# Query-key products over 128 rows with zeroed query rows, in place of products over 64 rows

## Chip, core and metric

The kernel runs on one NeuronCore of a Trainium2 chip, as one program. The metric is the device time of an execution in microseconds (us). The core has five engines with a queue each: PE (TensorE, matrix products; its weight loads are shown as PEld), DVE (VectorE), ACT (ScalarE), POOL (GpSimd) and SP (SyncE, which issues the transfers here). They meet by semaphores only.

## What is computed

Three transformer layers in a row over 512 tokens of width 1024, all in float32. The first two have the same form: a norm, an input projection, two kinds of attention side by side, an output projection, and a gated feed-forward block. The third mixes stick-breaking attention with a gated recurrence. What matters here are the query-key products:

```python
# differential attention: 4 heads, each with 2 maps m of width 64
logits = jnp.einsum('bqhmd,bkhmd->bhmqk', qi, k) * scale
p = softmax(where(causal, logits, NEG_INF))
p = p[:, :, 0] - lam * p[:, :, 1]
# forgetting attention: 8 heads of width 64, with a decay added to the logits
logits = jnp.einsum('bqhd,bkhd->bhqk', qi, k) * scale + decay
# stick-breaking attention, third layer: 8 heads of width 64
z = jnp.einsum('bhtd,bhsd->bhts', qb, kb) * scale
```

A head of width 64 fills half of the 128 partitions. The two maps of a differential head, and two neighbouring stick-breaking heads, lie above each other in one 128-row tile.

## The kernel before

Each engine has its own program, written out by hand, and its order is the order of its queue. Projections are made of three float32r products for each tile (`three`, lines 1291 to 1296): weights come by DMA into `raw`, ACT rounds them into `w_hi`, POOL subtracts into `w_lo`, and PE multiplies. This stream fills PE nearly everywhere.

**Attention of the first two layers** (`attention1` on PE, ACT and DVE). First 24 items are transposed (`items1`, `transpose_item`, line 1440): for each of four differential heads a query item into `QAT` and a key item into `KAT`, then queries and keys of the eight forgetting heads, with 66 rows each (64 and two for the decay). ACT takes the even items, the queries, out of PSUM (line 649), DVE the odd ones (line 1002). Six banks of PSUM rotate, and PE waits for an item's evacuation before it uses its bank again; after item 7 come the forget gate's sums.

Then 64 units (`units1`) run as a pipeline. The first 32 are differential, in the order head, block `i` of 128 queries, map `m`; the other 32 are forgetting, in the order head, block. At step `u` PE does three things in this order: it transposes the probabilities of unit `u - 5` (line 1489, only for `m == 1` in differential heads); it makes the query-key product of unit `u` (line 1501, `128 * (i + 1)` columns) and adds the causal mask to it with a bf16 product of the identity (line 1503); and it multiplies the transposed probabilities of unit `u - 6` by the values (line 1513). A differential query-key product takes partitions `64 * m` to `64 * m + 64` of both operands; the mask, the transposes and the value products take all 128, and a forgetting query-key product takes 66. For each unit DVE finds the maxima (line 1023), ACT takes the exponentials (line 673) and copies the transposed probabilities to SBUF (line 660), and DVE joins the two maps (lines 1030 to 1033) and scales the output (line 1018). The query-key products rotate over four banks.

**Stick-breaking attention** lies inside the input projection of the third layer. `SIDE` lists what is woven into each quarter lap of the projection: eight turned items (`items2`: queries to `QST`, keys to `KST`), then 32 units (`units2`) of a head and a block of keys. Each unit's query-key product (line 1576) takes 64 partitions of both operands and `512 - 128 * j` columns; it stands between products of the projection, which take 128.

Of the kernel before, what the change touches and what calls it, by code (L numbers as in the profile page):

```python
# [25 lines left out]
ALU = mybir.AluOpType  # L26
ACT = mybir.ActivationFunctionType
AX = mybir.AxisListType

P = 128  # L30
SEQ = 512
# [7 lines left out]
HD = 64  # L39
# [93 lines left out]
def build(nc, x, positions, attn_pre_g, w_in, forget_bias, lam_q1, lam_k1, lam_q2, lam_k2, diff_sub_g,  # L133
# [4 lines left out]
    with ctx:  # L138
        def sb(name, shape, dt=F32, scope=ctx):
            return scope.enter_context(nc.sbuf_tensor(name, shape, dt))  # L140
# [16 lines left out]
        G = sb("G", [P, D])  # L157
        gcol = sb("gcol", [P, 10, KD])
        qkg = sb("qkg", [P, 2])
        cs = sb("cs", [P, 2, T, ROT])  # L160
        fw = sb("fw", [P, DEPTH, KD, 16], F32R)
        fbias = sb("fbias", [P, DEPTH, 8])
# [30 lines left out]
        def at2(a, *dims):  # L193
            return view(R2, a, dims)
# [12 lines left out]
        QA = at2(0, T, CW)  # L207
        KA = at2(2048, T, CW)
# [2 lines left out]
        QB = at2(6160, T, 8, 66)  # L211
        KB = at2(8272, T, 8, 66)
        VB = at2(10384, T, 8, 65)
        QAT = at2(12464, 4, SEQ)
        KAT = at2(14512, 4, SEQ)
        prob = at2(16560, PROBS, SEQ)
        probT = at2(20144, 2, SEQ)
# [6 lines left out]
        YG_down = at1(0, T, D)  # L224
        junk_down = at1(4096, T, CW)

        QST, KST = at2(4096, 4, SEQ), at2(6144, 4, SEQ)
        VS = at2(8192, T, CW)
        QS, KS = at2(10240, T, CW), at2(12288, T, CW)
        SQ2 = at2(15872, T, CW)  # L230
# [110 lines left out]
        items1 = []  # L341
        for h in range(4):
            cols = slice(h * P, (h + 1) * P)
            items1 += [(QA[:, :, cols], P, QAT[:, h, :], HD ** -0.5), (KA[:, :, cols], P, KAT[:, h, :], 1.0)]
        for h in range(8):
            items1 += [(QB[:, :, h, :], 66, QBT[0:66, h, :], HD ** -0.5), (KB[:, :, h, :], 66, KBT[0:66, h, :], 1.0)]
        items2 = []
        for h in range(4):
            cols = slice(h * P, (h + 1) * P)
            items2 += [(QS[:, :, cols], P, QST[:, h, :], qkg[:, 0:1]), (KS[:, :, cols], P, KST[:, h, :], qkg[:, 1:2])]  # L350

        units1 = [("diff", (h, m), i) for h in range(4) for i in range(T) for m in range(2)]
# [178 lines left out]
        def _(act):  # L532
# [96 lines left out]
            nc.scalar.activation(cs[:, :, :, :], ang[:, 4:6], ACT.Sin).then_inc(trig_done, 1)  # L629
            act.preload_act_table_set(EXP_TABLE)  # L630

            def attention1(l):
                stage = f"in{l}"

                with act.Fori(2 if l == 0 else 1, LAPS[stage]) as lap:
                    hi_lap(stage, LAP0[stage] + lap)
                hi_first(f"out{l}")

                act.wait_ge(f_mm, l + 1)
                nc.scalar.activation(f_rows, PS[0:16, 0, :], ACT.Copy).then_inc(f_copied, 1)  # L640
                act.wait_ge(f_biased, l + 1)
                link(nc.scalar.activation(fy[:, 1], fy[:, 0], ACT.Abs))
                link(nc.scalar.activation(fy[:, 1], fy[:, 1], ACT.Exp, scale=-1.0))
                nc.scalar.activation(fy[:, 1], fy[:, 1], ACT.Ln, bias=1.0).then_inc(f_log, 1)

                for n, (src, rows, dst, scale) in enumerate(items1):
                    if n % 2 == 0:
                        act.wait_ge(tr_mm, len(items1) * l + n + 1)
                        nc.scalar.activation(dst, PS[0:rows, 2 + n % 6, :], ACT.Copy, scale=scale).then_inc(tr_act, 1)

                b, bo, bj = len(units1) * l, n_out * l, n_join * l
                for u in range(len(units1) + TURN):
                    v = u - TURN
                    if v >= 0 and has_output[v]:
                        i = units1[v][2]
                        n = outputs(v)
                        act.wait_ge(pt_mm, bo + n)
                        if bo + n > 2:
                            act.wait_ge(o_mm, bo + n - 2)
                        nc.scalar.activation(probT[:, n % 2, 0:P * (i + 1)], PS[:, 4 + n % 2, 0:P * (i + 1)],  # L660
                                             ACT.Copy).then_inc(pt_ev, 1)
                    if u < len(units1):
                        kind, (h, m), i = units1[u]
                        act.wait_ge(max_done, b + u + 1)
                        if u >= PROBS and has_output[u - PROBS]:
                            act.wait_ge(pt_mm, bo + outputs(u - PROBS))
                        elif u >= PROBS:
                            act.wait_ge(joined, bj + joins(u - PROBS + 1))
                        elif l and u == 0:
                            act.wait_ge(pt_mm, bo)  # L670

                        sums_to = dict(accum_out=dsum[:, (u // 2) % 8, m:m + 1]) if kind == "diff" else {}
                        nc.scalar.activation(prob[:, u % PROBS, 0:P * (i + 1)], PS[:, u % 4, 0:P * (i + 1)], ACT.Exp,
                                             bias=nmax[:, u % 4:u % 4 + 1], **sums_to).then_inc(exp_done, 1)
                    if u == DIFF_ROOT:
                        act.wait_ge(ss_ready, l + 1)
                        first_root(16, 2 * HD)
# [61 lines left out]
                nc.scalar.activation(w_hi[:, r], raw[:, r], ACT.Copy).then_inc(hi_ready, 1)  # L739

            def turn_side(n):
                src, rows, dst, scale = items2[n]
                if n % 2 == 0:
                    act.wait_ge(tr_mm, 2 * len(items1) + n + 1)
                    nc.scalar.activation(dst, PS[:, 4 + n % 4, :], ACT.Copy, scale=scale).then_inc(tr_act, 1)

            def sb_side(u):
                v = u - 3
# [95 lines left out]
        def _(dve):  # L844
            V = nc.vector
# [67 lines left out]
            for l in range(DEPTH):  # L913
                link(V.tensor_scalar(gcol[:, 3 * l + 1, 0:1], gcol[:, 3 * l + 1, 0:1], 1.0 - LAM_INIT[l], None, ALU.mult))
                V.tensor_copy(gcol[:, 3 * l + 1, 1:4], gcol[:, 3 * l + 1, 0:1].to_broadcast([P, 3]))
            V.tensor_scalar(qkg[:, 0:1], qkg[:, 0:1], HD ** -0.5, None, ALU.mult)
            link(V.tensor_copy(fw[:, :, :, 0:8], fw_raw))
            V.tensor_tensor(fw[:, :, :, 8:16], fw_raw, fw[:, :, :, 0:8].bitcast(F32), ALU.subtract).then_inc(fw_done, 1)

# [369 lines left out]
        def _(pe):  # L1289
# [153 lines left out]
            def attention1(l):  # L1443
# [33 lines left out]
                for u in range(len(units1) + PRODUCT):  # L1477
                    v = u - TURN
                    if 0 <= v < len(units1) and has_output[v]:
                        i = units1[v][2]  # L1480
                        n = outputs(v)
                        if units1[v][0] == "diff":
                            pe.wait_ge(joined, bj + joins(v))
                        else:
                            pe.wait_ge(exp_done, b + v + 1)
                        if bo + n > 2:
                            pe.wait_ge(pt_ev, bo + n - 2)
                        for j in range(i + 1):
                            last = nc.tensor.transpose(PS[:, 4 + n % 2, j * P:(j + 1) * P],  # L1489
                                                       prob[:, v % PROBS, j * P:(j + 1) * P], ident[:, :])  # L1490
                        last.then_inc(pt_mm, 1)
                    if u < len(units1):
                        kind, (h, m), i = units1[u]
                        tok, upto = slice(i * P, (i + 1) * P), P * (i + 1)
                        if kind == "diff":
                            q, kk = QAT[64 * m:64 * m + 64, h, tok], KAT[64 * m:64 * m + 64, h, 0:upto]
                        else:
                            q, kk = QBT[0:66, h, tok], KBT[0:66, h, 0:upto]
                        if b + u >= 4:
                            pe.wait_ge(exp_done, b + u - 3)  # L1500
                        mm(PS[:, u % 4, 0:upto], q, kk, start=True, stop=False)  # L1501

                        mm(PS[:, u % 4, upto - P:upto], ident_b[:, :], causal_b[:, :], start=False, stop=True).then_inc(s_mm, 1)  # L1503
                    v = u - PRODUCT
                    if v >= 0 and has_output[v]:
                        kind, (h, m), i = units1[v]
                        n = outputs(v)
                        pe.wait_ge(pt_ev, bo + n)
                        if bo + n > 2:
                            pe.wait_ge(o_norm, bo + n - 2)  # L1510
                        for j in range(i + 1):
                            vals, width = (VA[:, j, h * P:(h + 1) * P], P) if kind == "diff" else (VB[:, j, h, :], HD + 1)
                            last = mm(PS[:, 6 + n % 2, 0:width], probT[:, n % 2, j * P:(j + 1) * P], vals,  # L1513
                                      start=j == 0, stop=j == i)
                        last.then_inc(o_mm, 1)
# [50 lines left out]
            def sb_steps(u):  # L1566
# [3 lines left out]
                if u < len(units2):  # L1570
                    h, j = units2[u]
                    n = SEQ - P * j
                    rows = slice(64 * (h % 2), 64 * (h % 2) + 64)
                    if u >= 2:
                        pe.wait_ge(sp_done, u - 1)
                    mm(PS[:, 4 + u % 2, 0:n], KST[rows, h // 2, j * P:(j + 1) * P], QST[rows, h // 2, j * P:SEQ],  # L1576
                       start=True, stop=True).then_inc(z_mm, 1)
                yield
                v = u - 2
# [168 lines left out]
```

## Time and profile before

| | us |
|---|---|
| median of 3 runs | 2375.33 |
| the three runs | 2368.23, 2375.33, 2383.04 |
| the profiled execution, device time | 2381.19 |
| its span in the profile | 2379.4 |
| differential units, first layer | 173.4 to 220.1 |
| differential units, second layer | 872.3 to 938.2 |
| stick-breaking units | 1508 to 1672 |

A profile names groups of instructions by line, engine and operands; "64*128 64x512" on a PE line is a product that contracts over 64 rows, with 512 moving columns. A float32 product appears as two records ("x2"). The ends of PE's records are modelled, so lengths are read here from one start to the next start. The granted clock is TensorE's clock as a share of its full 2.4 GHz: 1.00 is 2.4 GHz and 0.50 is 1.2 GHz.

### The profile page before, as it was taken

What the parts mean: (1) busy time and instruction counts of PE and PEld (TensorE: products, weight loads), DVE (VectorE), ACT (ScalarE), POOL (GpSimd) and SP (SyncE); (2) the same over time, 40 slices, a digit from 0 to 9 for tenths busy, and PEclk for the clock granted to TensorE, in tenths of its full rate; (3) what the DMA queues carried; (4) which work ended last, traced back from release to release, by engine and by line L of the source; (5) the groups of instructions that cost most, each with busy time, mean ns of one, the idle gap of its engine ahead of it and who ended that gap; (6) DMA issues with size and microseconds to landing.
All of it is one profiled execution on the core that took longest, in us unless ns stands there. A gap on an engine that the chain in (4) does not pass through costs nothing.

```text
span 2379.4 us, 27399 instructions
## 1 busy us (share of the span) xinstructions
PE 2282.4 (96%) x10268; PEld 1775.5 (75%) x10268; DVE 716.9 (30%) x1374; ACT 736.9 (31%) x1217; POOL 842.7 (35%) x390
## 2 busy tenths in 40 slices
PE   7999999999989999999999999999798899999999
PEld 6876778888877865778888877777566677888887
DVE  5126442112022035542122023444466432212200
ACT  4135442222232134442222223444322243222211
POOL 3430134444434420134444434323334233444442
PEclk9998999999999986999999999999999999999999
DMA  5320023233232310023323322211111122332332
GB/s 162 97 63 1 28 80 98 88 97 93 93 97 80 89 44 1 19 81 97 97 89 97 92 92 74 62 45 53 39 43 44 45 75 77 96 97 88 97 93 93
DMA packets 138734, 178.20 MB, mean 75 GB/s; under 512 B 19856, under 2 KB 87696, under 8 KB 138640
## 3 DMA queue, kind: packets, MB, share of 16 engines
q1 hardware_dynamic: 137024, 175.25, 24.5%
q10 hardware_dynamic: 1616, 1.64, 0.2%
q8 instruction: 65, 1.06, 0.2%
q14 instruction: 29, 0.24, 0.0%
HBM read 174.76 MB, written 2.10 MB: 74 GB/s over the span
## 4 chain that ended last, share of the span: by engine, by line
PE 40%; issue 36%; POOL 18%; DVE 3%; ACT 1%; DMA 1%; POOLq 0%; SPq 0%; ACTq 0%; DVEq 0%
POOL w_lo L475 18%; PE PS L1294 8%; PE PS L1295 8%; PE PS L1296 8%; PE PS L1501 4%; PE PS L1513 3%; PE PS L1588 1%; DVE R L1206 1%; PE PS L1663 1%; PE PS L1489 1%; PE PS L1576 1%; PE PS L1440 1%; PE PS L1300 1%; PE PS L1602 1%; PE PS L1503 1%
## 5 line engine op out<-in xcount | busy, mean ns | idle before, releaser
L475 POOL TENSOR_TENSOR w_lo<-raw,w_hi 128x1024 fp32r<-128x1024 f32 (+1 forms) x288 | 676.9, 2351 | 1068.6 <-ACT w_hi L550 1068.6
L550 ACT ACTIVATE w_hi<-raw 128x1024 fp32r<-128x1024 f32 (+1 forms) x291 | 303.2, 1042 | 1075.5 <-DMA raw<-in_w_up 329.5
L1294 PE MATMUL PS<-xt_hi,w_hi 128*128 128x512 f32 x1120 | 450.9, 403 | 3.4 <-DVE xt_lo L886 3.4
L1295 PE MATMUL PS<-xt_lo,w_hi 128*128 128x512 f32 x1120 | 445.1, 397 | 0.0
L1296 PE MATMUL PS<-xt_hi,w_lo 128*128 128x512 f32 x1120 | 444.5, 397 | 0.0
L1294 PE MATMUL PS<-w_hi,xt_hi 128*128 128x512 f32 x928 | 389.3, 419 | 11.7 <-DVE xt_lo L886 8.4
L1295 PE MATMUL PS<-w_lo,xt_hi 128*128 128x512 f32 x928 | 370.7, 399 | 0.0
L1296 PE MATMUL PS<-w_hi,xt_lo 128*128 128x512 f32 x928 | 370.5, 399 | 0.0
L1294 PEld LDWEIGHTS PS<-xt_hi,w_hi 128*128 128x128 f32 x1120 | 211.7, 189 | 60.0 <-issue 10.8
L1296 PEld LDWEIGHTS PS<-xt_hi,w_lo 128*128 128x128 f32 x1120 | 211.8, 189 | 51.3
L1295 PEld LDWEIGHTS PS<-xt_lo,w_hi 128*128 128x128 f32 x1120 | 212.0, 189 | 48.4
L1084 DVE TENSOR_TENSOR h_tmp<-silu_g,PS 128x512 f32<-128x512 f32 x66 | 45.4, 687 | 581.6 <-ACT silu_g L710 580.5
L1294 PEld LDWEIGHTS PS<-w_hi,xt_hi 128*128 128x128 f32 x928 | 177.2, 191 | 58.1 <-issue 17.5
L1294 PE MATMUL PS<-w_hi,ht_hi 128*128 128x512 f32 x528 | 209.2, 396 | 5.6 <-POOL w_lo L475 5.6
L1296 PEld LDWEIGHTS PS<-w_hi,xt_lo 128*128 128x128 f32 x928 | 176.7, 190 | 43.2
L1296 PE MATMUL PS<-w_hi,ht_lo 128*128 128x512 f32 x528 | 208.5, 395 | 0.0
L1295 PE MATMUL PS<-w_lo,ht_hi 128*128 128x512 f32 x528 | 208.5, 395 | 0.0
L1295 PEld LDWEIGHTS PS<-w_lo,xt_hi 128*128 128x128 f32 x928 | 177.4, 191 | 37.2 <-issue 2.2
L469 POOL TENSOR_TENSOR w_lo<-raw,w_hi 128x1024 fp32r<-128x1024 f32 x40 | 99.0, 2476 | 133.1 <-ACT w_hi L739 125.4
L1294 PEld LDWEIGHTS PS<-w_hi,ht_hi 128*128 128x128 f32 x528 | 99.0, 187 | 32.1 <-POOL w_lo L475 8.2
L1296 PEld LDWEIGHTS PS<-w_hi,ht_lo 128*128 128x128 f32 x528 | 99.0, 187 | 24.2
L1501 PE MATMUL PS<-R 64*128 64x256 f32 (+7 forms) x256 | 115.3, 538 | 1.7 <-DVE R L1002 0.9
(215 smaller groups left out, 2136.5 us busy)
## 6 DMA issues: line engine op xcount, KB each, us to landing
raw<-in_w_in SPq DMA_DIRECT2D x92, 512.0 KB, 3.7
raw<-in_w_gate SPq DMA_DIRECT2D x88, 256.0 KB, 2.8
raw<-in_w_up SPq DMA_DIRECT2D x88, 256.0 KB, 3.0
raw<-in_w_down SPq DMA_DIRECT2D x40, 512.0 KB, 3.8
raw<-in_w_out SPq DMA_DIRECT2D x24, 512.0 KB, 3.8
raw<-in_w_ffn_gate SPq DMA_DIRECT2D x44, 256.0 KB, 2.8
raw<-in_w_ffn_up SPq DMA_DIRECT2D x44, 256.0 KB, 3.0
raw<-in_w_ffn_down SPq DMA_DIRECT2D x20, 512.0 KB, 3.8
```

The costliest lines, as they stand in the source:

```text
L469: nc.gpsimd.tensor_tensor(w_lo[:, r], raw[:, r], w_hi[:, r].bitcast(F32), ALU.subtract).then_inc(lo_ready, 1)
L475: nc.gpsimd.tensor_tensor(w_lo[:, r, 0:subs, :], raw[:, r, 0:subs, :], w_hi[:, r, 0:subs, :].bitcast(F32), ALU.subtract).then_inc(lo_ready, 1)
L550: nc.scalar.activation(w_hi[:, r, 0:subs, :], raw[:, r, 0:subs, :], ACT.Copy).then_inc(hi_ready, 1)
L1084: V.tensor_tensor(h_tmp[:, :], silu_g[:, j, :], PS[:, 4 * s + 2 + j, :], ALU.mult).then_inc(h_mul, 1)
L1206: V.tensor_reduce(hg_at[:, v % 2, :], hg_a.rearrange("p l t -> p t l"), AX.X, ALU.add).then_inc(a_sum, 1)
L1294: mm(out_, a_hi, b_hi, start=start, stop=False)
L1295: mm(out_, a_hi, b_lo, start=False, stop=False)
L1296: return mm(out_, a_lo, b_hi, start=False, stop=stop)
L1300: ins = nc.tensor.transpose(PS[:, 4 + k % 4, t * P:(t + 1) * P], SOURCE[stage][:, t, k * P:(k + 1) * P], ident[:, :])
L1440: last = nc.tensor.transpose(PS[0:rows, bank, t * P:(t + 1) * P], src[:, t, :], ident[:, :])
L1501: mm(PS[:, u % 4, 0:upto], q, kk, start=True, stop=False)
L1513: last = mm(PS[:, 6 + n % 2, 0:width], probT[:, n % 2, j * P:(j + 1) * P], vals, start=j == 0, stop=j == i)
```

## The change

Every query-key product of the differential and stick-breaking heads takes all 128 partitions. The keys of both maps (or both heads) stay above each other as they are. The queries are kept twice, in two buffers: buffer `m` holds the queries of map or head `m` in its 64 rows and zeros in the others. The zeros come from the scale of the copy out of PSUM: `one_head` holds a column for each `m` with the scale in its own rows and 0.0 in the others, so ACT copies each query item twice, with a column each. That makes 4 more ACT copies of 128x512 in each of the first two layers and 4 more in the third. `one_head` is filled by DVE in the preparation at the start (five instructions in place of one). Each product keeps its number of columns and of weights.

```diff
+        one_head = sb("one_head", [P, 2, 2])
-        QAT = at2(12464, 4, SEQ)
+        QAT = (at2(12464, 4, SEQ), at2(23216, 4, SEQ))
-        QST, KST = at2(4096, 4, SEQ), at2(6144, 4, SEQ)
+        QST = (at2(4096, 4, SEQ), at2(24064, 4, SEQ))
+        KST = at2(6144, 4, SEQ)
-            items1 += [(QA[:, :, cols], P, QAT[:, h, :], HD ** -0.5), (KA[:, :, cols], P, KAT[:, h, :], 1.0)]
+            items1 += [(QA[:, :, cols], P, [q[:, h, :] for q in QAT], one_head[:, 0, :]), (KA[:, :, cols], P, KAT[:, h, :], 1.0)]
-            items2 += [(QS[:, :, cols], P, QST[:, h, :], qkg[:, 0:1]), (KS[:, :, cols], P, KST[:, h, :], qkg[:, 1:2])]
+            items2 += [(QS[:, :, cols], P, [q[:, h, :] for q in QST], one_head[:, 1, :]), (KS[:, :, cols], P, KST[:, h, :], qkg[:, 1:2])]
+            def turned_out(item, bank):
+
+                src, rows, dst, scale = item
+                if not isinstance(dst, list):
+                    return nc.scalar.activation(dst, PS[0:rows, bank, :], ACT.Copy, scale=scale)
+                for m in range(2):
+                    last = nc.scalar.activation(dst[m], PS[:, bank, :], ACT.Copy, scale=scale[:, m:m + 1])
+                return last
-                        nc.scalar.activation(dst, PS[0:rows, 2 + n % 6, :], ACT.Copy, scale=scale).then_inc(tr_act, 1)
+                        turned_out(item, 2 + n % 6).then_inc(tr_act, 1)
-                    nc.scalar.activation(dst, PS[:, 4 + n % 4, :], ACT.Copy, scale=scale).then_inc(tr_act, 1)
+                    turned_out(items2[n], 4 + n % 4).then_inc(tr_act, 1)
-            V.tensor_scalar(qkg[:, 0:1], qkg[:, 0:1], HD ** -0.5, None, ALU.mult)
+            link(V.memset(one_head[:, :, :], 0.0))
+            for m in range(2):
+                rows = slice(HD * m, HD * m + HD)
+                link(V.memset(one_head[rows, 0, m:m + 1], HD ** -0.5))
+                link(V.tensor_scalar(one_head[rows, 1, m:m + 1], qkg[rows, 0:1], HD ** -0.5, None, ALU.mult))
-                            q, kk = QAT[64 * m:64 * m + 64, h, tok], KAT[64 * m:64 * m + 64, h, 0:upto]
+                            q, kk = QAT[m][:, h, tok], KAT[:, h, 0:upto]
-                    rows = slice(64 * (h % 2), 64 * (h % 2) + 64)
-                    mm(PS[:, 4 + u % 2, 0:n], KST[rows, h // 2, j * P:(j + 1) * P], QST[rows, h // 2, j * P:SEQ],
+                    mm(PS[:, 4 + u % 2, 0:n], KST[:, h // 2, j * P:(j + 1) * P], QST[h % 2][:, h // 2, j * P:SEQ],
```

## Rows read from the trace of the kernel before

**Rows 1.** page, section 2: granted TensorE clock in 40 slices of the span, tenths of full speed.

```profile
PEclk9998999999999986999999999999999999999999
```

**Rows 2.** windows by stage; columns: length, busy us per engine, granted clock, DMA share, GB/s.

```profile
173.40:220.10 46.70, 46.25 (x191) 25.65 (x192) 29.53 (x86) 23.38 (x75) 0.00 (x0) 0.85 0.00 1
872.30:938.20 65.90, 65.84 (x191) 35.47 (x192) 30.36 (x86) 24.00 (x75) 0.00 (x0) 0.56 0.00 1
220.10:270.00 49.90, 48.98 (x355) 39.31 (x353) 33.71 (x111) 29.86 (x72) 7.63 (x5) 1.00 0.00 1
...
1508.00:1672.00 164.00, 164.00 (x729) 115.83 (x729) 68.11 (x148) 72.23 (x143) 51.18 (x48) 1.00 0.17 49
```

**Rows 3.** windows of 1 us, PE only: where the granted clock falls and rises.

```profile
178.00:179.00 1.00, 1.00 (x4) 0.70 0.00 0
...
192.00:193.00 1.00, 1.00 (x5) 0.97 0.00 0
...
874.00:875.00 1.00, 1.00 (x4) 0.86 0.00 0
...
932.00:933.00 1.00, 1.00 (x2) 0.63 0.00 0
```

**Rows 4.** timeline of PE: start us, length us; differential heads, first layer, full clock.

```profile
197.98 0.48 PE L1501 MATMUL PS<-R 64*128 64x128 f32 x2
198.39 0.23 PE L1503 MATMUL PS<-causal_b,ident_b 128*128 128x128 bf16 x1
198.55 0.48 PE L1501 MATMUL PS<-R 64*128 64x128 f32 x2
...
205.98 0.27 PE L1489 MATMUL PS<-ident,R 128*128 128x128 f32 x1
206.18 1.12 PE L1501 MATMUL PS<-R 64*128 64x512 f32 x2
...
209.11 0.48 PE L1501 MATMUL PS<-R 64*128 64x128 f32 x2
```

**Rows 5.** the same timeline, forgetting heads (66 rows), full clock.

```profile
225.40 0.39 PE L1501 MATMUL PS<-R 66*128 66x128 f32 x2
225.62 0.22 PE L1503 MATMUL PS<-causal_b,ident_b 128*128 128x128 bf16 x1
225.68 0.28 PE L1489 MATMUL PS<-ident,R 128*128 128x128 f32 x1
225.79 0.60 PE L1501 MATMUL PS<-R 66*128 66x256 f32 x2
```

**Rows 6.** timeline of PE, differential heads, second layer, half clock.

```profile
884.45 0.79 PE L1501 MATMUL PS<-R 64*128 64x128 f32 x2
885.17 0.29 PE L1503 MATMUL PS<-causal_b,ident_b 128*128 128x128 bf16 x1
...
903.95 0.79 PE L1501 MATMUL PS<-R 64*128 64x128 f32 x2
```

**Rows 7.** timeline of PE, stick-breaking product between projection products.

```profile
1561.52 0.49 PE L1576 MATMUL PS<-R 64*128 64x128 f32 x2
1561.93 0.50 PE L1294 MATMUL PS<-xt_hi,w_hi 128*128 128x512 f32 x1
```

**Rows 8.** timeline of all engines at the end of a head, first layer.

```profile
197.32 0.23 PE L1503 MATMUL PS<-causal_b,ident_b 128*128 128x128 bf16 x1
...
198.99 0.37 ACT L660 ACTIVATE R<-PS 128x256 f32<-128x256 f32 x1
...
199.42 0.71 PE L1513 MATMUL PS<-R 128*128 128x128 f32 x4 [0.22 <-ACT R L660]
```

**Rows 9.** timeline, evacuation of the first eight transposed items, first layer.

```profile
162.30 2.04 ACT L649 ACTIVATE R<-PS 128x512 f32<-128x512 f32 x4
...
162.61 2.47 DVE L1002 TENSOR_SCALAR R<-PS 128x512 f32<-128x512 f32 x4
```

**Rows 10.** timeline, evacuation of the last turned query item before stick-breaking.

```profile
1505.25 0.69 ACT L745 ACTIVATE R<-PS,qkg 128x512 f32<-128x512 f32 x1 [2.96 <-PE PS L1440]
```

More of the change, by code:

```diff
@@ L644, in attention1 @@
                 nc.scalar.activation(fy[:, 1], fy[:, 1], ACT.Ln, bias=1.0).then_inc(f_log, 1)
-                for n, (src, rows, dst, scale) in enumerate(items1):
+                for n, item in enumerate(items1):
                     if n % 2 == 0:
                         act.wait_ge(tr_mm, len(items1) * l + n + 1)
-                        nc.scalar.activation(dst, PS[0:rows, 2 + n % 6, :], ACT.Copy, scale=scale).then_inc(tr_act, 1)
+                        turned_out(item, 2 + n % 6).then_inc(tr_act, 1)
                 b, bo, bj = len(units1) * l, n_out * l, n_join * l
@@ L741, in turn_side @@
             def turn_side(n):
-                src, rows, dst, scale = items2[n]
                 if n % 2 == 0:
                     act.wait_ge(tr_mm, 2 * len(items1) + n + 1)
-                    nc.scalar.activation(dst, PS[:, 4 + n % 4, :], ACT.Copy, scale=scale).then_inc(tr_act, 1)
+                    turned_out(items2[n], 4 + n % 4).then_inc(tr_act, 1)
             def sb_side(u):
```

## The prediction

> **What bounds the kernel now.** I read the page's row of granted clock first. [rows 1] Most slices stand at 9; the drops that last are slice 4 (8) and slices 15 and 16 (8 and 6) of 40, each 59.5 us long. They fall in the differential units of the two layers. Then I read the windows by stage. [rows 2] The differential units take 46.7 us in the first layer at a mean clock of 0.85, and 65.9 us in the second at 0.56: the same 32 units, the same 191 PE instructions, 19 us apart. PE is busy in nearly all of both, while DVE is busy for 29.5 and ACT for 23.4 of the 46.7 us. So PE sets the pace, and in part its clock. The forgetting units behind them run at 1.00, and so does the whole stick-breaking stretch, where PE is busy for 164.00 of 164 us: there every nanosecond taken from PE's stream is taken from the end.
>
> The windows of one microsecond date the clock. [rows 3] A slice whose mean is 0.70 holds 0.6 us at the 0.50 level, so the clock fell at 178.4 and, from the 0.97, rose at 192.1. In the second layer (0.86 and 0.63) it fell at 874.7 and rose at 932.7. PE was at half clock for 13.7 and 58.0 us. Both falls come within 5 us of the first differential product, when there are query-key products and masks and hardly anything between them. Both rises come amid differential units that are like the ones before.
>
> Last I read PE's timeline, which gives the price of one 64-row product.
>
> **The change part by part.** *Full clock, differential.* From a 64-row product of 128 columns to its mask is 0.41 us; from the mask to the next 64-row product 0.16; from a transpose to one 0.20. [rows 4] In the forgetting heads the same steps take 0.22, 0.06 and 0.11. [rows 5] Those products have the same columns and type, the same mask behind them, and differ in their 66 rows. So a 64-row product costs 0.19 us on its way out and 0.10 on its way in, say 0.30 together.
>
> The change makes all products 128-row ones. I price them as the 66-row ones; the other bound is that they keep the 0.30 (the third rival below). The Trainium skill, "TensorEngine Tiling (Array Packing)", Key Properties, states that changing the tiling mode drains the TensorE; by it 128-row products among 128-row ones have no drain left and the bound falls away. The trace agrees in that the extra time lies at both borders of a 64-row product. A unit then saves 0.30, a head of eight units 2.4 of its 11.13 us [rows 4], a layer of 32 units 9.6.
>
> A rule that speaks against the change: "TensorE: Matmul & The Clock Gate", Part 3 of the Trainium skill, says that small products in distinct row groups run at once. If the two maps did so before, the change would end it and lose half of a head's eight products: 2.2 us, by 0.22 for 128 columns, and 18 in all. The trace shows none of it: the second map's product starts 0.16 us after the mask, which waits for the first. [rows 4]
>
> *What takes the place of the drains.* PE isn't far ahead of the others at the end of a head. After the 512-column pair a value product waited for ACT's copy: the mask began at 197.32, the copy ran from 198.99, the product began at 199.42. [rows 8] That chain (maximum, exponential, copy) is 2.1 us and doesn't shorten. In front of that product PE has two 128-column units and thereby two drains, 0.6 us, that vanish and come back as waiting. Hence 1.8 saved a head in place of 2.4; I take 9.3 us for a head. Bounds: 8.7 if the chain hides, and some 10 if DVE, with 29.5 us of work a layer against 31.4 for PE, delays other units too.
>
> *The clock.* A head at half clock takes 19.50 us [rows 6] against 11.13, so 43% of the time at half clock is loss: 5.9 us of 13.7 and 24.9 us of 58.0. Taken off, the stages are 40.8 and 41.0 us; that they agree backs the reading. What will the clock do after? Forgetting units, without drains, never lost it in 50 us. [rows 2] It fell only where 64-row products made up most of PE's work. After the change that first stretch is denser and full-height. I take full clock in both layers; the other bound is the same half-clock time as now. The skill's page "TensorE: Matmul & The Clock Gate", Part 1, says that the gate follows how busy the array is. The trace agrees only if busy isn't the record's sense, since PE's busy share was 1.00 in the very slices of the falls. [rows 3]
>
> At full clock a stage is then 41.0 - 9.6 + 4 x 0.6 = 33.8 us. The first layer saves 46.7 - 33.8 = 12.9, the second 65.9 - 33.8 = 32.1.
>
> *Stick-breaking.* A 64-row product of 128 columns holds PE for 0.41 us until the projection's next product. [rows 7] That is the 0.19 again over 0.22, and I take the 0.10 of the entry with it: 0.30 x 32 = 9.6 us. PE is busy throughout, so all of it reaches the end. Bounds: 6, if the side chain on DVE and ACT then holds PE at some units, and 10.
>
> *What is added.* In each of the first two layers ACT has four more copies of 0.51 us. [rows 9] Its first eight items' share then ends at 162.30 + 8 x 0.51 = 166.4 rather than 164.3, DVE's at 165.1. What is late next is the bank of item 0, freed 0.5 us later, for which PE's item 6 waits, and the gate's sums behind it. DVE's 165.1 hides part of that: 0.4 us a layer, 0.8 together; nothing if it is all hidden, 2.04 a layer if none. In the third layer each extra copy is 0.6 to 0.7 us, and ACT was idle for 2.96 us before such a copy [rows 10]: nothing, and 4 x 0.69 = 2.8 without that cover. ACT's rounding of weights queues behind it, but the rounding runs three slots ahead of PE. The five small DVE instructions at the start lie before a copy that PE needs only a lap later: nothing; some 2 us if the next copy were due. No transfer is added or moved.
>
> *Sum.* 12.9 + 32.1 + 9.6 - 0.8 = 53.8 us. From the profiled execution's 2381.2 that leaves 2327.4. The median was 5.9 us lower than this execution. I don't subtract that: the runs differ by 15 us with the same work, most likely in their time at half clock, which the forecast takes away anyway. If it lay elsewhere, the result would be 2321.5. **Forecast 2327.**
>
> **Rivals.**
> *The clock behaves as now.* The falls came early and the rises at no visible event, which speaks for a habit of the stage. The forgetting stretches at 1.00 speak against. At half clock a product's way out is 0.72 us [rows 6], against 0.44 for twice 0.22: 0.28, with 0.10 in, 0.38 a unit. The second layer saves 32 x 0.38 = 12.2, the first 8.5 (32 x 0.30, 0.7 more for nine units at half clock, 1.8 less for the waits of three heads); with 9.6 - 0.8 that is 29.5. Here the median is the right base: 2375.3 - 29.5 = 2346.
> *Waiting takes the place of every drain in the differential stages*, because DVE's and ACT's chains bind. For it: the wait in [rows 8] and DVE's 29.5 us. Against it: they leave 4 us in 33.8. A stage is 41.0, so 2327.4 + 2 x 7.2 = 2342.
> *The price isn't that of 64 rows*, but of something that both kernels share, such as the wider value products; then only the added copies are left: 2376. Against it, stick-breaking shows the same 0.41 without them. [rows 7]
> *Slower.* With waits in PE's stream in place of drains, the array is less active, the clock falls in both differential stages and stays down in the forgetting ones. The stages are 65.9 - 12.2 = 53.7 each, which costs 7.0 and saves 12.2; with 8.8 more, 14.0 saved. The two forgetting stretches of 50 us grow by 75%: +75. That gives 2381.2 - 14.0 + 75 = 2442. It decides from about 19 us of forgetting work at half clock. Against it: those stretches never fell, and aren't changed.
>
> **How the numbers follow.** Full clock 0.71, clock as now 0.14, waits for drains 0.08, no price 0.03, slower 0.04. The likeliest case's own range is 2318 to 2337: 8.7 or 10 us a head (-5, +6), the added copies (up to +5), stick-breaking (+3), the median's offset (-6). The range 2319 to 2349 takes in the waiting case and most of the clock case. A measurement of this kernel tells about 1% from no change, here 24 us, so faster ends at 2351.6. Faster: 0.71, two thirds of the clock case (0.09) and 0.07 of the waits: 0.87. Within 1%: 0.05 + 0.01 + 0.03 = 0.09. Slower: 0.04.
>
> **What would show it.** Line 1501 as 128*128 with 0.22 us from product to mask and 0.06 behind it; granted clock 1.00 over both stages; both stages near 34 us and equal; more waits of the value products for ACT's copy; 32 stick-breaking products with 0.22 in place of 0.41 and the stretch near 154 us. It is wrong if the 1 us windows still show 0.50 for tens of microseconds, if product to mask stays at 0.41, or if the evacuation before the units grows by over 1 us.

## The result, and the profile after

| | before | changed |
|---|---|---|
| median, us | 2379.18 (4 runs, 2368.23 to 2384.3) | 2279.82 (4 runs, 2276.68 to 2281.47) |
| span of the profiled execution, us | 2379.4 | 2279.2 |
| differential units, first layer | 46.73 | 34.29 |
| differential units, second layer | 65.84 | 34.28 |
| stick-breaking, first product to last | 149.75 | 137.05 |

The ratio is 0.958, with a 95% interval of 0.9538 to 0.9621: faster, by 99 us. The forecast was 2327, and its range ended at 2319. The direction was right and the size wrong: 54 us were foreseen, and some 45 more came.

The page of the changed kernel, section 2, shows the clock's slices answering to [rows 1]:

```profile
PEclk9999999999999999999999999999999999999999
```

The drops in slices 4, 15 and 16 are gone. The windows by stage of the changed kernel (length, busy us of PE, PEld, DVE, ACT and POOL with counts, granted clock, DMA share, GB/s) answer to [rows 2]; the last is the stick-breaking stretch and the work just behind it:

```profile
169.60:203.90 34.30, 32.00 (x191) 22.71 (x192) 28.59 (x86) 22.31 (x74) 0.00 (x0) 1.00 0.00 1
841.80:876.10 34.30, 31.98 (x191) 22.71 (x192) 28.58 (x86) 22.30 (x74) 0.00 (x0) 1.00 0.00 1
1433.60:1585.00 151.40, 151.40 (x731) 120.23 (x730) 68.60 (x148) 71.66 (x143) 51.97 (x48) 1.00 0.17 53
```

Both differential stages now take the same 34.3 us at full clock. In the stick-breaking stretch PE is busy without a break, as before, and from its first product to its last it takes 137.05 us in place of 149.75. The timeline of PE in the second differential head of the first layer (start us, length us) answers to [rows 4]:

```profile
174.85 0.22 PE L1517 MATMUL PS<-causal_b,ident_b 128*128 128x128 bf16 x1
...
175.40 0.39 PE L1515 MATMUL PS<-R 128*128 128x128 f32 x2
175.63 0.22 PE L1517 MATMUL PS<-causal_b,ident_b 128*128 128x128 bf16 x1
175.68 0.44 PE L1515 MATMUL PS<-R 128*128 128x128 f32 x2
175.96 0.22 PE L1517 MATMUL PS<-causal_b,ident_b 128*128 128x128 bf16 x1
176.94 0.71 PE L1527 MATMUL PS<-R 128*128 128x128 f32 x4 [0.76 <-ACT R L671]
...
182.41 0.27 PE L1503 MATMUL PS<-ident,R 128*128 128x128 f32 x1
182.52 1.02 PE L1515 MATMUL PS<-R 128*128 128x512 f32 x2
183.38 0.22 PE L1517 MATMUL PS<-causal_b,ident_b 128*128 128x128 bf16 x1
...
184.91 0.39 PE L1515 MATMUL PS<-R 128*128 128x128 f32 x2
```

From product to mask 0.23 us in place of 0.41, and for 512 columns 0.86 in place of 1.06; behind a mask 0.05 in place of 0.16; behind a transpose 0.11 in place of 0.20. A head takes 9.51 us, not 11.13. The value product waits longer: 0.98 us from the mask's start at 175.96 to its own at 176.94, where it was 0.45 before (198.97 to 199.42). The chain behind it is as long as it was, 2.09 us from the mask at 174.85 and 2.10 in [rows 8].

The two stages (12.4 and 31.6 us), the stick-breaking stretch (12.7) and the added copies (1.1 us lost) come to some 56 us. Most of the rest lies in a place where the diff changes no instruction. Four products of the first input projection, long before the first attention, in the kernel before (first fence) and in the changed kernel (second fence), from the timeline of PE:

```profile
100.06 0.40 PE L1296 MATMUL PS<-w_hi,xt_lo 128*128 128x512 f32 x1
100.29 0.39 PE L1294 MATMUL PS<-w_hi,xt_hi 128*128 128x512 f32 x1
100.53 0.40 PE L1295 MATMUL PS<-w_lo,xt_hi 128*128 128x512 f32 x1
100.76 0.39 PE L1296 MATMUL PS<-w_hi,xt_lo 128*128 128x512 f32 x1
```

```profile
100.00 0.39 PE L1310 MATMUL PS<-w_hi,xt_lo 128*128 128x512 f32 x1
100.23 0.39 PE L1308 MATMUL PS<-w_hi,xt_hi 128*128 128x512 f32 x1
100.46 0.39 PE L1309 MATMUL PS<-w_lo,xt_hi 128*128 128x512 f32 x1
100.69 0.39 PE L1310 MATMUL PS<-w_hi,xt_lo 128*128 128x512 f32 x1
```

From the first start to the fourth are 0.70 us before and 0.69 after, in rounded figures. Over longer stretches (some 100 products between 100 and 125 us, between 400 and 425, and between 600 and 620) the step is 0.2334 us before and 0.2267 after, in every kind of projection: 3%. There are 7728 such products, so all of them together could be worth 52 us.

### The profile page after: what moved, and what is told of

Its sections match the earlier page's. It is cut to its first block, busy times and chain, and to the rows that moved or that the text cites. A ratio compares the mean times of both kernels' runs of the same rounds, so it can differ in the third digit from the quotient of the medians.

```text
span 2279.2 us, 27415 instructions
## 1 busy us (share of the span) xinstructions
PE 2175.2 (95%) x10268; PEld 1763.4 (77%) x10268; DVE 716.1 (31%) x1378; ACT 741.2 (33%) x1229; POOL 843.8 (37%) x390
## 3 DMA queue, kind: packets, MB, share of 16 engines
q8 instruction: 65, 1.06, 0.2%
## 4 chain that ended last, share of the span: by engine, by line
PE 38%; issue 36%; POOL 19%; DVE 4%; ACT 2%; DMA 1%; POOLq 0%; SPq 0%; ACTq 0%; DVEq 0%
POOL w_lo L477 18%; PE PS L1308 8%; PE PS L1310 8%; PE PS L1309 8%; PE PS L1515 3%; PE PS L1527 2%; PE PS L1601 2%; DVE R L1220 1%; PE PS L1676 1%; PE PS L1503 1%; PE PS L1454 1%; PE PS L1589 1%; PE PS L1615 1%; PE PS L1314 1%; DMA raw<-in_w_out 1%
## 5 line engine op out<-in xcount | busy, mean ns | idle before, releaser
L1308 PE MATMUL PS<-xt_hi,w_hi 128*128 128x512 f32 x1120 | 446.0, 398 | 3.4 <-DVE xt_lo L896 3.4
L1310 PE MATMUL PS<-xt_hi,w_lo 128*128 128x512 f32 x1120 | 438.2, 391 | 0.0
L1309 PE MATMUL PS<-xt_lo,w_hi 128*128 128x512 f32 x1120 | 437.9, 391 | 0.0
L1309 PE MATMUL PS<-w_lo,xt_hi 128*128 128x512 f32 x928 | 365.6, 394 | 0.0
L1309 PEld LDWEIGHTS PS<-w_lo,ht_hi 128*128 128x128 f32 x528 | 99.2, 188 | 20.2
```

Source lines behind the costliest of these rows:

```text
L1308: mm(out_, a_hi, b_hi, start=start, stop=False)
L1309: mm(out_, a_hi, b_lo, start=False, stop=False)
L1310: return mm(out_, a_lo, b_hi, start=False, stop=stop)
```

## Experiment 1: where the operands lie

```diff
 e1_pad32, against the kernel before
         qkg = sb("qkg", [P, 2])
+        pad = sb("pad", [P, 8])
 e3_pad64, against the kernel before
+        pad = sb("pad", [P, 16])
 e2_unshifted, against the changed kernel
-        one_head = sb("one_head", [P, 2, 2])
 ...
         R2 = sb("R2", [P, 28672])
+        one_head = sb("one_head", [P, 2, 2])
 e4_pad64, against the changed kernel
         one_head = sb("one_head", [P, 2, 2])
+        pad = sb("pad", [P, 16])
```

> The kernel before with one unused 32-byte tensor behind qkg, which moves all tensors behind it by 32 bytes, as one_head does in the changed kernel; xt_hi, xt_lo, ht_hi, ht_lo and the attention buffers then start at a multiple of 64 bytes instead of 32 past one. No instruction differs. Placement theory (a float32r product takes 0.2334 us from start to start in the trace of before and 0.2267 in the trace of after because of the start of its operands in SBUF): 0.2267 here, some 45 us off the kernel before, about 2334 us, and the half-clock stretches stay. Rival (the 64-row products slow all of PE's stream, or the query copies matter): 0.2334 and no change, 2379 us.

> The changed kernel with one_head placed behind all other tensors, so that every other tensor starts where it starts in the kernel before. Placement theory: products of the projections back at 0.2334 us, differential stages at 34 us and full clock, stick-breaking some 10 us shorter than before: about 2326 us, which is the forecast of the sum. Rival: 2280 us as the changed kernel.

> The kernel before with an unused 64-byte tensor behind qkg: all starts move by 64 bytes and stay 32 past a multiple of 64. If what counts is the start within 64 bytes: 0.2334 us and 2379 us, as before. If any move, or a start within 128 bytes, counts: another value than 0.2334 (the place in 128 bytes goes from 96 to 32).

> The changed kernel with 64 more bytes in front of the operands: their start goes from 0 to 64 within 128 bytes and stays a multiple of 64. If 64 bytes are what counts: 0.2267 us and 2280 us, as the changed kernel. If 128 bytes count: slower, up to 0.2334 us and 2326 us.

| kernel | median, us | ratio to before, 95% interval | step of a projection product, us |
|---|---|---|---|
| e1_pad32 | 2339.15 | 0.9804 (0.9717 to 0.9891) | 0.2267 |
| e2_unshifted | 2322.26 | 0.9736 (0.9671 to 0.9801) | 0.2334 |
| e3_pad64 | 2384.17 | 0.9986 (0.9956 to 1.0017) | 0.2334 |
| e4_pad64 | 2313.24 | 0.9692 (0.9626 to 0.9757) | 0.2334; 0.2289 in the first half of the feed-forward |

Before them the kernel before had 2385.45 us as its median of 13 runs in that session. e1_pad32 has no changed instruction and is 46 us faster, 26 to 68 by its interval. The interval is so wide because the executions of both kernels differ in their time at half clock; at the same mean clock of 0.975 they take 2326.35 and 2368.67 us, and at 0.965 they take 2346.07 and 2391.15: 42 and 45 us apart. e2_unshifted has the whole change and no move, and takes 2322 us, 5 from the forecast's sum of 2327. The windows over its two differential stages show that the stages don't depend on the move (34.29 us each between the first product and the first forgetting one; the columns are length, PE's busy us and instructions, granted clock, DMA share, GB/s):

```profile
173.90:208.20 34.30, 32.02 (x192) 1.00 0.01 1
859.80:894.10 34.30, 32.02 (x192) 1.00 0.00 1
```

So the change brings 57 to 63 us by its products (against 2379 and 2385), and 42.4 us (2322.26 - 2279.82) by a tensor of 16 bytes. The placement theory stands, the rival falls. That it is less than 52 us is due mostly to the third layer's input projection: its 1440 products gain 1.3 us from first to last (some 4 without the changed kernel's longer time at half clock there, an estimate by the forecast's 43%) and not 9.6. Between two of them within the stick-breaking stretch the step is 0.2325 us in e2_unshifted and 0.2307 in the changed kernel; why the move helps less there isn't known.

The stretches of the profiled executions also close the sum of e2_unshifted: 12.4 + 31.6 for the stages, 12.4 for stick-breaking, 1.0 lost by the copies are 55.4 us, and outside the stages the clock was at half for 71.4 us before and for 64.6 in e2_unshifted, which by the forecast's 43% is an estimated 2.9 more. Together they are 58.3, and the spans are 2379.4 and 2321.2, 58.2 apart.

Another rival is that engines which write the weights while PE reads them get in its way. It falls by the traces: projection steps during which ACT, DVE and POOL are all idle average 0.2333 us in the kernel before (1716 steps) and 0.2268 in the changed one (1641).

But e4_pad64, where the operands still start at a multiple of 64, is slow again, so a start within 64 bytes isn't the rule.

## Experiment 2: what about the place counts

Three more kernels, all from the changed one. In e6_xt128 and s1_place `R2` is 2048 bytes shorter, in a part that nothing uses.

```diff
 e5_all32
+        pad = sb("pad", [P, 8])
         X = sb("X", [P, T, D])
 e6_xt128
         one_head = sb("one_head", [P, 2, 2])
+        pad = sb("pad", [P, 32])
 s1_place
         one_head = sb("one_head", [P, 2, 2])
+        pad = sb("pad", [P, 64])
 ...
         R1 = sb("R1", [P, 2 * KD * SEQ])
+        pad_2 = sb("pad_2", [P, 32])
```

> The changed kernel with an unused 32-byte tensor in front of X, so that the weights (w_hi, w_lo) and the activations (xt, ht) both start 32 bytes past a multiple of 128. If the distance between the two operands of a product is what counts, it is unchanged: 0.2267 us a product and 2280 us. If each operand's own start counts: 0.2334 us or more, 2326 us or more (and more if a second misaligned operand adds to the first).

> The changed kernel with the activations 128 bytes further on, at 81920, a multiple of 16384 (R2 is made 2048 bytes shorter, in a part that nothing uses). If a multiple of 128 is all that counts: 0.2267 us and 2280 us. If larger multiples or the distance to the weights count: another value; 0.2157 us, the 512 columns at 2.4 GHz and nothing else, would give some 2200 us.

> The changed kernel with other places of the activations. Counted as the distance from the weights within 512 bytes, the fast kernels have 256, the slow ones 224, 288, 320 and 384. Here xt is at 0 and ht (the second projection of the feed-forward blocks) at 128. If 0 is as good as 256: products with xt at 0.2267 us. If 256 is the only good one: 0.2334 everywhere and about 2320 us. If the distance counts within 256 bytes, 0 and 256 are the same.

In e5_all32 both operands lie 32 bytes further on, off every larger multiple, and the kernel is as fast as the changed one: 2277.83 us (2 runs), step 0.2267. In e6_xt128 the activations start at a multiple of 16384, and it is slow: 2318.37 us, 0.2323 to 0.2335. An operand's own alignment is thus not what counts; the distance between the two is. In s1_place `xt` and `ht` (the activations of the feed-forward's second half) have different distances: 2289.12 us (2 runs). Its step is 0.2267 with `xt` and 0.2325 with `ht`, and 1584 products with `ht` times 0.0058 are 9.2 us. It lies 9.3 above the changed kernel; with two runs 6 us apart, so close a match is luck, but the steps are clear.

All results, by the distance between the starts of weights and activations within 256 bytes (tiles inside the tensors start at multiples of 512 bytes, so it is the same for every product):

| distance, bytes | where | step, us |
|---|---|---|
| 0 | changed kernel, e1_pad32, e5_all32; `xt` in s1_place | 0.2267 |
| 32 | e3_pad64 | 0.2334 |
| 64 | e4_pad64 | weights moving: 0.2334; weights held in the array, activations moving: 0.2289 |
| 128 | e6_xt128; `ht` in s1_place | 0.2323 to 0.2335 |
| 224 | kernel before, e2_unshifted | 0.2334 |

Of the five distances only 0 is fast. In e4_pad64 it matters which operand moves; counted from the held operand to the moving one, 64 is 64 where the activations move and 192 where the weights do. That this direction is what makes the difference wasn't tested. That 256 is the length that counts, rather than 512, rests on the changed kernel (256 within 512 bytes) and s1_place (0 within 512), which are equally fast. The Trainium skill, "TensorE: Matmul & The Clock Gate", Part 2, says that TensorE reads its two operands through two independent ports, and that loading the next tile's weights doesn't take bandwidth from the running matmul. Here a weight load runs beside every product, and the step depends on the distance between the two operands by 3%, which two reads without any effect on each other wouldn't show; there the measurement differs. That it is these two reads that meet is inferred, and where they would meet wasn't measured; the mechanism stays open.

## Experiment 3: what brings the clock down, and what a border costs

All new kernels here have the operands at distance 0. Two leave the mask out of the differential units (so their differential attention isn't causal, and their result is another), e10_half_drains has 64 rows for the first map only, e11_diff64 for both maps, and e12_pairs puts the two 64-row products side by side with both masks behind them.

```diff
 e8_nomask64 (from e1_pad32) and e9_nomask128 (from the changed kernel)
-                        mm(PS[:, u % 4, 0:upto], q, kk, start=True, stop=False)
-                        mm(PS[:, u % 4, upto - P:upto], ident_b[:, :], causal_b[:, :], start=False, stop=True).then_inc(s_mm, 1)
+                        last = mm(PS[:, u % 4, 0:upto], q, kk, start=True, stop=kind == "diff")
+                        if kind != "diff":
+                            last = mm(PS[:, u % 4, upto - P:upto], ident_b[:, :], causal_b[:, :], start=False, stop=True)
+                        last.then_inc(s_mm, 1)
 e10_half_drains
-                            q, kk = QAT[m][:, h, tok], KAT[:, h, 0:upto]
+                            rows = slice(0, 64) if m == 0 else slice(0, 128)
+                            q, kk = QAT[m][rows, h, tok], KAT[rows, h, 0:upto]
 e11_diff64
+                            rows = slice(64 * m, 64 * m + 64)
+                            q, kk = QAT[m][rows, h, tok], KAT[rows, h, 0:upto]
 e12_pairs (units w = u, u + 1 at each even differential u)
+                        for w in pair:
 ...
+                                rows = slice(64 * m, 64 * m + 64)
+                                q, kk = QAT[m][rows, h, tok], KAT[rows, h, 0:upto]
 ...
+                            mm(PS[:, w % 4, 0:upto], q, kk, start=True, stop=False)
+                        for w in pair:
+                            mm(PS[:, w % 4, upto - P:upto], ident_b[:, :], causal_b[:, :], start=False, stop=True).then_inc(s_mm, 1)
```

> The kernel before with 32 unused bytes (as e1_pad32), and without the causal mask's product in the differential units, which leaves the causal masking of differential attention out. In the first six units nothing but 64-row products is left, with no change of height between them. If the time at the borders of a 64-row product is a change of height: none between these products, 0.22 us or less for 128 columns from start to start. If products in the two halves of the rows run at once, the second map's product starts well under 0.2 us after the first's. Clock: if the standing of the array at the borders brings it down, it stays at 1.00 in this stretch; if the half-height products do, it falls again within 5 us of the first unit.

> The changed kernel without the causal mask's product in the differential units (this leaves the causal masking of differential attention out): the control for e8_nomask64 with 128-row products. Clock 1.00 through both differential stages, 0.22 us from one 128-column product to the next; 32 masks of 0.06 us fewer in each layer, so at most 4 us less than the changed kernel, about 2278 us.

> The changed kernel, but the first map's products (m == 0) of the differential heads contract over 64 rows again; the second map's keep 128. Same operand places. Half of the borders come back: a layer's stage is 34.3 us plus 16 x 0.30 = 39.1 at full clock, some 1 or 2 us less where they fall into a wait that is there anyway: 37 to 39. Clock theory (the fall comes from the half-height products and their borders together, and needs most of PE's work to be of that kind): stays at 1.00, about 2289 us. Rival (any 64-row products at the start of the stage bring it down): falls within 5 us of the first unit, stages of 45 us and more, 2300 us or above.

> The changed kernel, but all differential products contract over 64 rows again; the stick-breaking products, the query copies and the places stay. Stages back at 55 to 66 us with the clock at 0.50 for most of them, and the stick-breaking stretch 12.3 us shorter than in e1_pad32 (149.4 us from its first product to its last, there; 137.1 in the changed kernel): 2339 - 12 + 1 = 2328 us. If the query copies or the place of the query buffers had kept the clock up, the stages would be 41 us and the kernel at 2294.

> The changed kernel, but the differential products contract over 64 rows again, and the two maps' products of a unit pair follow each other directly, with both masks behind them (e8_nomask64 showed such pairs at once: 1.06 us for two of 512 columns). Same result as the reference. Per head PE then has four pairs at the time of one product each and four drains of 0.3 in place of eight products: 8.7 - 2.2 + 1.2 = 7.7 us, below what the chain of DVE and ACT allows (9.5 a head in the changed kernel). If the clock holds: stages 31 to 34 us and 2274 to 2280 us. If half-height products bring it down, as for 2 us in 4 in e8_nomask64: 35 to 45 us a stage, 2285 to 2300.

| kernel | first stage, us | second stage, us | median, us |
|---|---|---|---|
| kernel before | 46.73 | 65.84 | 2379.18 |
| e1_pad32 | 57.09 | 65.86 | 2339.15 |
| e3_pad64 | 55.49 | 64.35 | 2384.17 |
| e11_diff64 | 55.50 | 41.04 | 2316.13 |
| e10_half_drains | 37.87 | 37.87 | 2289.50 (2 runs) |
| changed kernel, e5_all32, e6_xt128, s1_place | 34.29 | 34.29 | |
| e8_nomask64 | 33.57 | 30.46 | 2291.08 (2 runs) |
| e9_nomask128 | 31.99 | 32.00 | 2279.22 (2 runs) |
| e12_pairs | 33.46 | 31.90 | 2280.84 |

The control e9_nomask128 came out within 1.3 us of its 2278, e10_half_drains in its 37 to 39 us a stage, and both stages of e12_pairs in 31 to 34; e11_diff64 missed its 2328.

*The price of a border.* The windows over the two stages of e11_diff64 (PE only):

```profile
171.20:226.70 55.50, 55.27 (x191) 0.69 0.00 1
863.90:905.00 41.10, 40.42 (x192) 1.00 0.00 1
```

The second stage ran wholly at full clock, and took 41.04 us. That is the 41.0 that the forecast had worked out for a 64-row stage without loss of clock. The change takes 6.75 us from it, by its products alone. Half of the borders (e10_half_drains) cost 3.58 of these 6.75.

*The clock.* e11_diff64 has the same instructions in both stages; one lost the clock and the other didn't. With all differential products at 64 rows and a mask behind each, the clock fell in seven of eight stages (before, e1_pad32, e3_pad64, e11_diff64). So 64-row products make the fall possible and don't enforce it. Its four runs reach from 2307.66 to 2323.62 us, while e2_unshifted, without 64-row products, stays within 3 us. The expectation of 2328 had both stages cold and missed by 12 us. In e10_half_drains, with 64-row products in every second unit, the clock stayed up in both stages:

```profile
170.80:208.60 37.80, 36.41 (x191) 1.00 0.00 1
846.60:884.50 37.90, 36.51 (x192) 1.00 0.00 1
```

The rival in its expectation falls: some 64-row products at the start of a stage aren't enough. No kernel with only 128-row and 66-row products lost the clock in these stages, in seven traces (changed, e2, e4, e5, e6, e9 and s1). e8_nomask64 lost it without a change of height inside a pair. Its windows from 182 us on, with PE waiting in between:

```profile
182.00:186.00 4.00, 2.53 (x19) 0.97 0.00 0
186.00:190.00 4.00, 4.00 (x19) 0.60 0.00 2
190.00:194.00 4.00, 3.32 (x21) 1.00 0.00 0
194.00:198.00 4.00, 3.21 (x17) 0.75 0.00 0
```

Its control e9_nomask128 waits as well, and stays at 1.00 in both stages. But it waits less, 0.98 us in a head against 1.47, because its products take longer. So waits of about 1 us don't bring the clock down here; whether the longer waits or the half-height products do it in e8_nomask64 isn't separated. Its second stage has the same waits and kept the clock, and the fall didn't come within 5 us of the first unit, as one branch of the expectation had it, but after 16.5. In the kernel before it is no matter of waits: up to the two falls PE is busy for 0.94 to 1.00 of every microsecond. What exactly is weighed isn't settled.

*Two halves at once.* The timeline of PE in e8_nomask64 shows a pair of 512-column products as one entry of four records, and in e9_nomask128 below it the same pair over 128 rows:

```profile
180.95 1.13 PE L1502 MATMUL PS<-R 64*128 64x512 f32 x4
182.01 0.49 PE L1515 MATMUL PS<-R 128*128 128x128 f32 x2
```

```profile
183.42 1.88 PE L1515 MATMUL PS<-R 128*128 128x512 f32 x4
185.14 0.38 PE L1528 MATMUL PS<-R 128*128 128x128 f32 x2
```

The pair takes 1.06 us in the first and 1.72 in the second. Two products in different halves of the rows do run at once when nothing stands between them. This is the rule of Part 3 of "TensorE: Matmul & The Clock Gate" in the Trainium skill that the prediction had weighed; it holds, and in the kernel before the mask between the maps kept it from working. e12_pairs uses it in a kernel with the full result:

```profile
184.05 1.13 PE L1518 MATMUL PS<-R 64*128 64x512 f32 x4
185.12 0.28 PE L1520 MATMUL PS<-causal_b,ident_b 128*128 128x128 bf16 x2
```

A pair costs 1.07 us where the changed kernel needs 1.83 with one mask between (182.52 to 184.35). Its second stage is 2.4 us shorter than the changed kernel's, the first only 0.8, with a mean clock of 0.95 there: it fell to half for 3.4 us at 177.9, behind a wait of 0.89. The value product waits for ACT's copy for as long as 1.35 us in a head, which takes most of the gain. As a whole it is no faster: 2280.84 against 2279.82. No kernel beat the changed one by more than the runs scatter.

## Why the prediction was wrong, step by step

**The drains in the differential stages: right, a little too high.** 0.19 out and 0.10 in came out as 0.18 to 0.20 and 0.09 to 0.11, and 128-row products cost what the 66-row ones did. Only the second product of a pair, directly behind a mask, still takes 0.28 us to its own mask (175.68 to 175.96) and not 0.22; no product of [rows 5] stands there. Without the wait a head saved 2.15 us where 2.4 were forecast, and a stage is 34.3 us where 33.8 were.

**What takes their place: right.** The named wait took back 0.53 us a head against a forecast 0.6, so a head takes 9.51 us against 9.3.

**The clock: right in its result.** It is at 1.00 in both stages after the change. The loss that was taken off is confirmed by a stage that happened not to have it (41.04). That the falls are a habit of the stage was too strong: e11_diff64 had one of two. The forecast's guess that the runs of before differ in their time at half clock is borne out. Its 27 executions beside the experiments reach from 2360 to 2401 us, at mean clocks of 0.980 to 0.960. Fitted over them, the time grows by 0.43 us for each us at half clock (worked out from the mean clock), which is the 43% that the forecast read from two heads. One reading of the unchanged-clock rival was off: six units of the first layer ran at half clock, not nine, which is 0.2 us.

**Stick-breaking: right mechanism, term too small.** 9.6 us were forecast for 32 products. At the same places 12.4 came (149.75 in the kernel before less 137.38 in e2_unshifted), 0.39 for each, and the move of the operands added 0.3. The step mis-sized is the price of the borders, 0.30 where it is 0.39. The price without a border was right. The timeline of the kernel before, which continues [rows 7], and of the changed kernel:

```profile
1561.19 0.40 PE L1296 MATMUL PS<-xt_hi,w_lo 128*128 128x512 f32 x1
1561.52 0.49 PE L1576 MATMUL PS<-R 64*128 64x128 f32 x2
1561.93 0.50 PE L1294 MATMUL PS<-xt_hi,w_hi 128*128 128x512 f32 x1
1562.27 0.40 PE L1295 MATMUL PS<-xt_lo,w_hi 128*128 128x512 f32 x1
```

```profile
1501.44 0.39 PE L1310 MATMUL PS<-xt_hi,w_lo 128*128 128x512 f32 x1
1501.68 0.38 PE L1589 MATMUL PS<-R 128*128 128x128 f32 x2
1501.82 0.48 PE L1308 MATMUL PS<-xt_hi,w_hi 128*128 128x512 f32 x1
1502.13 0.39 PE L1309 MATMUL PS<-xt_lo,w_hi 128*128 128x512 f32 x1
```

The forecast stopped at the start of the next projection product, 0.41 us behind the 64-row one. But that product is longer too: 0.34 us to the one behind it, where a projection product otherwise takes 0.23. So the borders cost 0.10 on the way in, 0.19 on the way out and 0.10 in the product behind. In the changed kernel the next start is only 0.14 us away, and the product there takes 0.31: the record starts early, and the 128-column product costs 0.22 in all, as forecast. Over the products of all four widths, from the start before to the second start behind, the difference between the kernel before and e2_unshifted is 0.39 to 0.40 us. The bounds had ended at 10, which was too near: they held only losses.

**The added copies: right.** From the first transpose to the first unit the first layer took 14.81 us before and takes 15.36; 0.4 was forecast, 0.55 came (0.53 in the second layer), and it is the wait for item 0's second copy:

```profile
159.28 1.09 PE L1454 MATMUL PS<-ident,R 128*128 128x128 f32 x8 [0.55 <-ACT R L640]
```

In the third layer nothing was forecast and nothing came: from the first product of its input projection to the first stick-breaking product are 75.5 us before and 75.4 in e2_unshifted.

**What failed: the step "What is added".** It listed copies, small DVE instructions and transfers, and not the 16 bytes of `one_head`, nor what their place moves. The sum had no term for it: 42 us by e2_unshifted against the changed kernel, and with it 2327 would have been 2285. No rival had it either. The trace of before alone doesn't show that 0.2334 us is a slow value, since it shows no other. That the move of 32 bytes went to the fast place was luck: from the same start a move of 64 (e3_pad64) brings nothing.

The part that the forecast did cover, 53.8 us, is 55.4 in e2_unshifted: the stages brought 1.0 less, stick-breaking 2.8 more and the copies 0.2 less. So the closeness of 2322 to 2327 is not a matter of large errors that cancel.

## What to carry to other kernels

A query product over half of the rows, between products over all of them, pays 0.3 to 0.4 us for its borders, and a stage full of them was at half clock for 14 to 58 us in seven of eight cases. Zeros in the unused rows cost nothing on PE. Read the price of such a border to the second start behind it, since the first can hide a part. If the halves can stand next to each other without anything between, they run at once instead, which pays if PE is what the stage waits for. Whenever a change adds or removes a tensor, look at the step of a product that it doesn't touch: a small pad in front of one operand is a cheap experiment, and here the place brought 42 of the 99 us.

## What the runs showed of the hardware that was not expected

A float32r product of 128x512, with a weight load for each, takes 0.2267 us where moving and held operand lie a multiple of 256 bytes apart in the partition, and 0.2289 to 0.2335 at the distances of 32, 64, 128 and 224 bytes; over this kernel it is 42 us. Absolute alignment, up to a multiple of 16384 bytes, didn't help. The stick-breaking stretch, where such products alternate with others, hardly noticed the move: 137.38 us in e2_unshifted and 137.05 in the changed kernel, from its first product to its last. And two float32 products of 64x512 in different halves of the rows take 1.06 us together when they are neighbours, but start 1.22 us apart (206.18 and 207.40 in the kernel before) when a 128-row mask of 0.06 us stands between them.
